# Projecting the gates in two token halves, with the sample's preparation dealt out between the tiles of the second

## The chip, the core and the metric

The kernel runs on one core of one Trainium2 chip. The metric is the device time of one execution in microseconds (us). A core has TensorE (PE: matrix products, its weight loads are shown as PEld), VectorE (DVE), ScalarE (ACT), GpSimd (POOL) and SyncE (SP), which only issues DMAs. Each engine works through its own queue in order and waits on semaphores. SBUF is the memory on the chip, PSUM the banks that TensorE writes.

## The reference, cut to what matters

The kernel computes one layer for a prompt of 2048 tokens and for a sample of 8 requests with one new token each. Both go through the same projection, and the sample then attends to a paged cache of 16,384 tokens.

```python
D_MODEL = 1024; SEQ = 2048; DEC_BATCH = 8; HEAD_DIM = 128; Q_LORA = 384; KV_LORA = 256; MLA_ROPE = 64; N_MEM = 256
IN_SIZES = (RET_W, RET_W, RET_W, Q_LORA, KV_LORA, MLA_ROPE, MEM_W, D_MIX)      # 512 512 512 384 256 64 512 1536

def project(h, pos, norm_g, w_in, qnorm_g, w_uq, w_uk, kvnorm_g):
    z = rms_norm(h, norm_g) @ w_in
    rq, rk, rv, cq, ckv, kpe, mq, gate = _split_cols(z, IN_SIZES)
    rq = rope(rq.reshape(B, T, RET_HEADS, HEAD_DIM), pos)
    rk = rope(rk.reshape(B, T, RET_HEADS, HEAD_DIM), pos) * (HEAD_DIM ** -0.5)
    q = jnp.einsum('btc,chd->bthd', rms_norm(cq, qnorm_g), w_uq)
    q_nope = q[..., :MLA_NOPE]
    q_pe = rope(q[..., MLA_NOPE:], pos)
    q_lat = jnp.einsum('bthd,chd->bthc', q_nope, w_uk)
    ckv = rms_norm(ckv, kvnorm_g)
    kpe = rope(kpe, pos)
    ...
# the sample: retention of one token per request, and memory attention over 256 rows per request
S = S * s_dec + k v^T ;  o = q S                     # state_ret (8, 4, 128, 128)
mem_o = mem_attend(mq, cache_mem_k[l], cache_mem_v[l])    # each (8, 256, 4, 128)
```

## The kernel before, in words

The work runs in stages, each a block in which all engines have their own program, with a barrier and a clearing of semaphores between two blocks (`Room.clear`, L82). The stages around the change are three.

**The projection** (`project`, L165 to L665). The prompt's rows stand turned in SBUF, split in a high part `xh` and a low part `xl`, each 128 x 8 x 2048 numbers, together 128 KB of each partition. The weights come in 17 stripes of 256 columns (`STRIPES`, L120): 3 and 2 stripes of the kind "N", 4 of the kind "R" (rotated), with 16 tiles each, and 8 of the kind "T" with 8 tiles each, of which 2 are memory queries and 6 are gates. A T tile is 128 columns of the weights by 512 tokens: 24 matmuls (L616), three products for each of 8 chunks. GpSimd loads the next stripe into `raw`, ScalarE copies its high part to `wh` (L404), VectorE subtracts for `wl` (L485). A tile goes to PSUM bank n % 4; ScalarE writes even tiles to `stage` (L421), VectorE odd ones (L517), and SyncE stores each pair (L332). In each stripe TensorE also projects the sample's 8 rows: `sample_rows`, a group of 16 matmuls (L631) after one tile and one of 2 (L638) some tiles later (`rows_at`, L138); VectorE copies the results out and SyncE stores them to `s_zs` (L339).

**The sample's preparation** (`sample_prepare`, L2370 to L2826), a block of its own. It reads `s_zs` back, normalises, rotates, projects the queries (`w_uq`, `w_uk`), builds the page indices and lets GpSimd gather the first step of the paged cache (L1802, L1804), adds k v^T to the states (`outer` on TensorE L2704, `new_state` on VectorE L2527), reads them with the queries (L2719), computes memory scores on VectorE (`spread` on TensorE L2712, `memory_scores` L2534 and L2537), their softmax, the memory values (L2819) and a head norm. All states (2 MB), memory keys (4 MB) and memory values (4 MB) are loaded whole.

**The sample's attention and the prompt's retention** (`sample_attention_and_retention`, from L1808), which starts with the tiles in `keep` (indices, queries, the first gathered rows).

Of the kernel before, what the change touches and what calls it, by code (L numbers as in the profile page):

```python
# [28 lines left out]
P = 128  # L29
# [24 lines left out]
class Count:  # L54


    def __init__(self, base=0):
        self.at = base
# [51 lines left out]
def rms_scale(dve, link, x, square, stat, n):  # L110
# [11 lines left out]
           + [("N", O_RV + c, SW) for c in range(0, W3, SW)] + [("T", NAT + c, SW) for c in range(0, TRN, SW)])  # L122
# [10 lines left out]
def tiles_of(stripe):  # L133

    return stripe[2] // P * (SEQ // 512) if stripe[0] == "T" else BLOCKS


def rows_at(s):  # L138

    return ROWS_AT if s == 0 else (1, 4)  # L140
# [24 lines left out]
def project(nc, t):  # L165
# [6 lines left out]
    with ExitStack() as ctx:  # L172
        r = Room(nc, ctx, "pj")
        xh = r.sb("xh", [P, KD, SEQ], F32R)
        xl = r.sb("xl", [P, KD, SEQ], F32R)
        raw = r.sb("raw", [P, 2, KD, SW])
        wh = [r.sb("wh0", [P, KD, SW], F32R)]
        wl = [r.sb("wl0", [P, KD, SW], F32R)]
        stage = r.sb("stage", [P, 2, 2, 512])
        xsT = r.sb("xsT", [P, KD, DEC])  # L180
        parts = r.sb("parts", [P, DEC])
        rows4 = r.sb("rows4", [P, SW])
        rows = r.sb("rows", [DEC, SW])
        kv = stage[:, :, :, :].rearrange("p b x n -> p b (x n)")
        mem_gain = kv[:, 1, :]
        with ExitStack() as early:
            def first(name, shape, dt=F32):
                return early.enter_context(nc.sbuf_tensor(f"pn_{name}", shape, dt))

            xmT = first("xmT", [P, KD, NMEM])  # L190
            kT = first("kT", [P, HEADS, NMEM])
            gain = first("gain", [P, D])
            x = first("x", [P, 4, D])
            ident = first("ident", [P, P])
            square = first("square", [P, D], mybir.dt.bfloat16)
            total = first("total", [P, 2 * PAIRS])
            half = first("half", [P, 2])
            stat = first("stat", [P, 2, 2, 2])
        wh.append(r.sb("wh1", [P, KD, SW], F32R))
        wl.append(r.sb("wl1", [P, KD, SW], F32R))  # L200
        rot = r.sb("rot", [P, 2, 2, HD + HD // 2])
        by_cos = r.sb("by_cos", [P, 2, HD])
        by_sin = r.sb("by_sin", [P, 2, HD])
        turned = r.sb("turned", [P, 2, 2, HD])
        decay = r.sb("decay", [P, 2 * HEADS])
# [3 lines left out]
        ps_row = r.ps("ps_row", [DEC, 512])  # L209
        (consts, mem_gain_in, gain_in, sum_ok, xn_ok, xT_ps, xm_ok, hi_ok, lo_ok, xs_ok, kv_out, w_hi, w_lo, mm_ok, clear_ok, row4_ps, row4_ok,  # L210
         row_ps, row_ok, row_out, ev_act, ev_dve, chain, mean_ok, root_ok, turned_ok, decay_in, parts_in, kT_out) = [r.sem(n) for n in (
            "consts mem_gain_in gain_in sum_ok xn_ok xT_ps xm_ok hi_ok lo_ok xs_ok kv_out w_hi w_lo mm_ok clear_ok row4_ps row4_ok "
            "row_ps row_ok row_out ev_act ev_dve chain mean_ok root_ok turned_ok decay_in parts_in kT_out").split()]
# [12 lines left out]
        TURNS = 2 * SAMPLE + 1  # L226

# [8 lines left out]
        with nc.Block() as block:  # L236
            @block.gpsimd
            def _(pool):
# [18 lines left out]
                for s, (kind, c0, w) in enumerate(STRIPES):  # L257
                    if s < 2:
                        pool.wait_ge(mm_ok, MEM_TILES - 2 + 2 * s)
                    else:  # L260
                        pool.wait_ge(w_lo, s - 1)
                        pool.wait_ge(row4_ps, s - 1)
                    pool.dma_start(raw[:, s % 2, :, 0:w], w_rows[:, :, c0:c0 + w]).then_inc(w_in[s % 2], 16)
                    for q in ((MEM_STRIPES + 1,), range(MEM_STRIPES + 2, PAIRS))[s] if s < 2 else ():
                        root_of(q)

            @block.sync
            def _(sp):
# [46 lines left out]
                for s, (kind, c0, w) in enumerate(STRIPES):  # L315
                    if s == 1:
# [4 lines left out]
                        load_rotation(1)  # L321
                    for n in range(first_tile[s], first_tile[s + 1], 2):
# [7 lines left out]
                        if kind == "T":  # L330
                            m, c = u // 4, u % 4
# [5 lines left out]
                        if u == rows_at(s)[1] // 2 * 2:  # L337
                            sp.wait_ge(row_ok, s + 1)
                            sp.dma_start(t["s_zs"][:, c0:c0 + w], rows[:, 0:w]).then_inc(row_out, 16)  # L339
# [5 lines left out]
                sp.wait_ge(row_out, 16 * len(STRIPES))  # L345
# [6 lines left out]
            def factor(s):  # L352
                return -MEM_SCALE if STRIPES[s][0] == "T" and STRIPES[s][1] < O_GATE else 1.0
# [16 lines left out]
            def _(act):  # L370
# [7 lines left out]
                def high_part(b):  # L378

                    for half in range(1 if b == SAMPLE else 2):  # L380
# [7 lines left out]
                        else:  # L388
                            act.copy(xh[:, chunk, (b - 2) * P:(b - 1) * P], ps_t[:, h % 2, :, :]).then_inc(hi_ok, 1)

                def early_tile(n):
                    act.wait_ge(mm_ok, n + 1)
                    to, w = early_target(n)
                    act.copy(to, ps[:, n % QUAD, 0:w]).then_inc(ev_act, 1)
# [11 lines left out]
                def tile(s, n):  # L406
# [10 lines left out]
                    elif n % 2 == 0:  # L417
                        stage_free(act, n)
                        act.wait_ge(mm_ok, n + 1)
                        w_tile = 512 if kind == "T" else w  # L420
                        act.activation(stage_view(n, w_tile), ps[:, n % QUAD, 0:w_tile], ACT.Copy, scale=factor(s)).then_inc(ev_act, 1)  # L421
# [26 lines left out]
                for s in range(1, len(STRIPES)):  # L448
                    if s + 1 < len(STRIPES):
                        split(s + 1)  # L450
                    for n in range(first_tile[s], first_tile[s + 1]):
                        tile(s, n)

            @block.vector
            def _(dve):
# [14 lines left out]
                def low_part(b):  # L470
                    for half in range(2):
                        h = 2 * (b - 2) + half
                        at = slice(half * HALF, (half + 1) * HALF), slice((b - 2) * P, (b - 1) * P)
                        dve.wait_ge(hi_ok, h + 1)
                        dve.tensor_tensor(xl[:, at[0], at[1]], ps_t[:, h % 2, :, :], xh[:, at[0], at[1]], ALU.subtract).then_inc(lo_ok, 1)
# [2437 lines left out]
```

## Time and profile before

| what | us |
|---|---|
| three runs | 2301.97 (median), 2296.97 to 2302.07 |
| the profiled execution | 2294.27, its span 2292.5 |
| last matmul of the projection starts | 861.57 |
| first instruction of the preparation's block | 866.63 |
| first instruction of the block after it | 942.36 |

Positions are us from the start of the span. The span is cut on the page into 40 slices of 57.3 us. PEclk is the granted clock of TensorE: 1.00 is 2.4 GHz, 0.50 is 1.2 GHz.

### The profile page before, as it was taken

To read this page: it belongs to the slowest core of one execution; us is meant where nothing else is said; L and a number is where in the kernel's file an instruction comes from. 1 tells how busy PE (TensorE), PEld (TensorE's weight loads), DVE (VectorE), ACT (ScalarE), POOL (GpSimd) and SP (SyncE) were. 2 spreads that over 40 slices of the span, in tenths; PEclk is the share of its full clock that TensorE was granted. 3 is DMA by queue.
4 is the path that set the end of the run, shared out by engine and by line. 5 is a ranking of instruction groups with operands and counts; after the bars stand their busy time and mean duration, and the time that the engine had idled before them with its cause. 6 is when DMAs were issued, how large, how long until landed. Compare 5 with 4: busy or idle time off the path is not lost. (4 is left out here: it accounts for less than half of the span.)

```text
span 2292.5 us, 48413 instructions
## 1 busy us (share of the span) xinstructions
PE 2124.3 (93%) x20401; PEld 1782.8 (78%) x20401; DVE 1278.5 (56%) x2736; ACT 653.1 (28%) x1478; POOL 223.9 (10%) x289
## 2 busy tenths in 40 slices
PE   7999999999999997599999999859899999899998
PEld 6999999997777775376677677648788888768886
DVE  4412444111111105599999999866577777655555
ACT  5311222100010001033333343434345545421110
POOL 1000000000000001122222222111222010000000
PEclk9999999999999995699999999979999999999999
DMA  7322332211112117799999999579997282154452
GB/s 255 112 74 78 100 99 89 83 61 65 65 65 83 46 47 245 295 364 363 369 378 371 374 366 377 202 252 308 349 212 137 48 148 99 50 191 138 160 161 83
DMA packets 185067, 421.94 MB, mean 184 GB/s; under 512 B 15072, under 2 KB 104320, under 8 KB 176664
## 3 DMA queue, kind: packets, MB, share of 16 engines
q0 software_dynamic: 44992, 234.56, 31.1%
q1 hardware_dynamic: 139872, 184.46, 24.0%
q8 instruction: 154, 2.52, 0.4%
q14 instruction: 49, 0.40, 0.1%
HBM read 325.48 MB, written 93.30 MB: 183 GB/s over the span
## 5 line engine op out<-in xcount | busy, mean ns | idle before, releaser
L618 PE MATMUL pj_ps<-pj_wh,pj_xh 128*128 128x256 f32 (+1 forms) x1152 | 326.1, 283 | 2.8 <-issue 2.8
L618 PE MATMUL pj_ps<-pj_wh,pj_xl 128*128 128x256 f32 (+1 forms) x1152 | 323.6, 281 | 0.0
L618 PE MATMUL pj_ps<-pj_wl,pj_xh 128*128 128x256 f32 (+1 forms) x1152 | 323.5, 281 | 0.0
L517 DVE TENSOR_SCALAR pj_stage<-pj_ps 128x256 f32<-128x256 f32 (+2 forms) x72 | 38.5, 535 | 483.1 <-PE pj_ps L616 314.2
L618 PEld LDWEIGHTS pj_ps<-pj_wh,pj_xh 128*128 128x128 f32 x1152 | 219.6, 191 | 10.6 <-issue 10.1
L2196 PE MATMUL sa_ps_s<-sa_turned,keep_q 128*32 128x128 f32 x5120 | 183.7, 279 | 47.5 <-DVE sa_turned L1972 44.2
L1972 DVE STREAM_TRANSPOSE sa_turned<-sa_nat 128x2048 f32<-128x2048 f32 x96 | 220.0, 2291 | 13.4 <-DMA sa_kp<-cache_kpe,keep_index 13.4
L618 PEld LDWEIGHTS pj_ps<-pj_wh,pj_xl 128*128 128x128 f32 x1152 | 219.7, 191 | 0.0
L618 PEld LDWEIGHTS pj_ps<-pj_wl,pj_xh 128*128 128x128 f32 x1152 | 219.7, 191 | 0.0
L616 PE MATMUL pj_ps<-pj_xh,pj_wh 128*128 128x512 f32 x512 | 202.7, 396 | 0.0
L616 PE MATMUL pj_ps<-pj_xl,pj_wh 128*128 128x512 f32 x512 | 201.0, 393 | 0.0
L616 PE MATMUL pj_ps<-pj_xh,pj_wl 128*128 128x512 f32 x512 | 200.9, 392 | 0.0
L2196 PEld LDWEIGHTS sa_ps_s<-sa_turned,keep_q 128*32 128x32 f32 x5120 | 132.8, 111 | 77.9 <-DVE sa_turned L1972 59.0
L421 ACT ACTIVATE pj_stage<-pj_ps 128x256 f32<-128x256 f32 (+2 forms) x72 | 34.1, 473 | 481.3 <-PE pj_ps L616 302.0
L1363 DVE TENSOR_TENSOR la_pl<-la_ps_p,la_ph 128x512 fp32r<-128x512 f32 (+1 forms) x144 | 88.4, 656 | 72.0 <-ACT la_ph L1409 72.0
L616 PEld LDWEIGHTS pj_ps<-pj_xh,pj_wh 128*128 128x128 f32 x512 | 96.1, 188 | 27.8 <-issue 6.9
L1400 ACT ACTIVATE la_row<-la_row,la_soft 128x128 f32<-128x128 f32 (+7 forms) x64 | 77.2, 1207 | 127.9 <-DVE la_soft L1350 127.9
L616 PEld LDWEIGHTS pj_ps<-pj_xl,pj_wh 128*128 128x128 f32 x512 | 96.1, 188 | 21.8
L616 PEld LDWEIGHTS pj_ps<-pj_xh,pj_wl 128*128 128x128 f32 x512 | 96.2, 188 | 21.0
L2220 PE MATMUL sa_ps_o<-sa_nat,sa_p_turned 128*16 128x256 f32 x1536 | 94.3, 379 | 4.4 <-issue 4.4
L1342 DVE CUSTOM_DVE_ANT_0 la_row<-la_ps_s,begin_causal 128x512 f32<-128x512 f32 (+3 forms) x160 | 92.3, 605 | 9.7 <-PE la_ps_s L1466 9.7
L1409 ACT CAST la_ph<-la_ps_p 128x512 fp32r<-128x512 f32 (+1 forms) x144 | 74.3, 565 | 39.5 <-PE la_ps_p L1479 38.6
(450 smaller groups left out, 4281.1 us busy)
## 6 DMA issues: line engine op xcount, KB each, us to landing
pj_raw<-w_in POOLq DMA_DIRECT2D x16, 1024.0 KB, 6.4
s_zn<-pj_stage SPq DMA_DIRECT2D x64, 256.0 KB, 2.2
s_zt<-pj_stage SPq DMA_DIRECT2D x32, 512.0 KB, 2.6
rm_z<-s_zn SPq DMA_DIRECT2D x16, 768.0 KB, 9.6
pn_x<-x_prompt SPq DMA_DIRECT2D x16, 512.0 KB, 3.8
s_k<-lp_st SPq DMA_DIRECT2D x16, 512.0 KB, 8.2
s_v<-lp_st SPq DMA_DIRECT2D x32, 256.0 KB, 5.3
s_qn<-lp_st SPq DMA_DIRECT2D x16, 512.0 KB, 5.1
```

The source lines that it names most:

```text
L421: act.activation(stage_view(n, w_tile), ps[:, n % QUAD, 0:w_tile], ACT.Copy, scale=factor(s)).then_inc(ev_act, 1)
L517: dve.tensor_scalar(stage_view(n, w_tile), ps[:, n % QUAD, 0:w_tile], factor(s), None, ALU.mult).then_inc(ev_dve, 1)
L616: mm = pe.matmul(ps[:, n % QUAD, :], wt[:, k, m * P:(m + 1) * P], of[:, k, c * 512:(c + 1) * 512], **flags)
L618: mm = pe.matmul(ps[:, n % QUAD, 0:w], of[:, k, u * P:(u + 1) * P], wt[:, k, 0:w], **flags)
L1342: dve.tensor_tensor_reduce(out=row[:, s, q, c * P:(c + w) * P], in0=ps_s[:, (at + n) % 3, 0:w * P], in1=m, scale=1.0, scalar=-3.0e38, op0= ...
L1363: dve.tensor_tensor(pl[:, n % RING, 0:w], ps_p[:, n % RING, 0:w], ph[:, n % RING, 0:w], ALU.subtract).then_inc(pl_ok, 1)
L1400: act.activation(row[:, s, q, 0:n], row[:, s, q, 0:n], ACT.Exp, bias=soft[:, s, q, 1:2], scale=MLA_SCALE, accum_out=soft[:, s, q, 2:3]).th ...
L1409: act.copy(ph[:, n % RING, 0:w], ps_p[:, n % RING, 0:w]).then_inc(ph_ok, 1)
L1972: dve.transpose(turned[:, s, a:z, :, :].rearrange("p c x q -> p x c q"), of.rearrange("p x (c q) -> p x c q", q=QR)).then_inc(t_ok, 1)
L2196: mm = pe.matmul(ps_s[j * QR:(j + 1) * QR, s, 0:TQ * QR], q32[:, u, c, :], turned[:, s, c, j * TQ:(j + 1) * TQ, :].rearrange("p x q -> p ( ...
L2220: mm = pe.matmul(ps_o[j * QR:j * QR + ROWS_Q, 0:KVL], p_turned[:, s, x, j, :], nat[g % DEEP][:, TQ * j + x, :], start=(x == 0), stop=(x == ...
```

## The change

The six gate stripes are projected twice over half of the tokens each: first all six for tokens 0 to 1023 (kind "T0", 4 tiles a stripe), then all six for tokens 1024 to 2047 (kind "T1"). So each gate stripe's weights are loaded and split twice. `xh` and `xl` are two tensors each, one per half; the first halves stand on the right side of SBUF and are given up when the T0 tiles are done. In that memory lie the tiles of the preparation, which is no block of its own any more: the class `SamplePrepare` has one method for each engine, called with k after tile k of the 24 T1 tiles ("slot" k). Tiles of T1 use two PSUM banks in turn, and the preparation the other six. The states are handled in two halves of 4 requests, and memory keys and values pass one request at a time through a ring of two buffers. The sample's gate rows are projected in T0, after tiles 0 and 2 of a stripe.

```diff
-           + [("N", O_RV + c, SW) for c in range(0, W3, SW)] + [("T", NAT + c, SW) for c in range(0, TRN, SW)])
+           + [("N", O_RV + c, SW) for c in range(0, W3, SW)] + [("T", O_MQ + c, SW) for c in range(0, W3, SW)]
+           + [(half, O_GATE + c, SW) for half in ("T0", "T1") for c in range(0, MIX, SW)])
...
-        xh = r.sb("xh", [P, KD, SEQ], F32R)
-        xl = r.sb("xl", [P, KD, SEQ], F32R)
+            xh, xl = [[front_half.enter_context(nc.sbuf_tensor(f"pj_{n}0", [P, KD, HALF_SEQ], F32R, side="right")),
+                       r.sb(f"{n}1", [P, KD, HALF_SEQ], F32R)] for n in ("xh", "xl")]
...
+        def bank_of(n):
+            return n % QUAD if n < late else late % QUAD // 2 * 2 + (n - late) % 2
...
                     if n >= QUAD:
-                        evacuated(pe, n - QUAD, free)
+                        evacuated(pe, n - 2 if n >= late + 2 else n - QUAD, free)
...
+                    if s >= LATE + 2:
+                        sample.pool(s - LATE - 2, pool)
...
-                        for i in range(2):
-                            evacuated(sp, n + i, staged)
+                        evacuated(sp, n, staged)
+                        if s >= LATE:
+                            sample.sync(n - late, sp)
+                        evacuated(sp, n + 1, staged)
...
                     for n in range(first_tile[s], first_tile[s + 1]):
                         tile(s, n)
-                        sample_rows(s, n - first_tile[s])
+                        if s >= LATE:
+                            sample.tensor(n - late, pe)
+                        else:
+                            sample_rows(s, n - first_tile[s])
...
+        if k == -1:
+            self.turned_over(sp)
+            self.zs_written(sp)
...
+        if 4 <= k <= 9:
+            sp.wait_ge(self.kq_ok, k - 3)
+            load_memory("cache_mem_k", k - 2)
+        if k == 5:
+            sp.wait_ge(self.cq_ps, 1)
+            sp.wait_ge(self.q4_ok, 2)
+            for n in range(QUADS):
+                for i in range(QUADS):
+                    sp.dma_start(self.q_in[i * QR:(i + 1) * QR, :, n, :], ...)
...
+        if 14 <= k <= 19:
+            sp.wait_ge(self.mo_ps, k - 13)
+            load_memory("cache_mem_v", k - 12)
...
+        if k == 1:                          # TensorE
+            self.banks_free(pe)
+            pe.wait_ge(self.ident_in, 16)
+            pe.wait_ge(self.cqn_ok, 1)
...
+        if 4 <= k <= 11:
+            spread(k - 4)
+        if k == 7:
+            pe.wait_ge(self.pick_in, 16)
+            pe.wait_ge(self.prod_ok, 1)
...
+            outer(0)
+            outer(1)
+        if k == 8:
+            outer(2)
+            outer(3)
+        if k == 9:
+            retention(0)
...
+        if 14 <= k <= 21:
+            memory_values(k - 14)
+        if k == 22:
+            pe.wait_ge(self.rows_ok, 2)
+            pe.wait_ge(self.cats_ok, 1)
+            turn_rows().then_inc(self.moT_ps, 1)
```

On TensorE the preparation's products stood together in a block of their own. Before (`sp_` names are tiles of the preparation, `sp_bank` its PSUM banks):

```order
L2763 MATMUL sp_bank<-keep_ident,sp_q_lat 128x128 x2
L2767 MATMUL sp_bank<-keep_ident,sp_qk 128x8 x4
L2712 MATMUL sp_bank<-sp_zs,sp_one_row 128x512
L2704 MATMUL sp_bank<-sp_zs,sp_k_only 128x128 x4
L2775 MATMUL sp_bank<-sp_psum,sp_pick 128x8 x4
L2704 MATMUL sp_bank<-sp_zs,sp_k_only 128x128 x4
L2712 MATMUL sp_bank<-sp_zs,sp_one_row 128x512
```

Now the same kinds stand between tiles; this is slot 7, the fullest, with the last two matmuls of tile 7 and the first of tile 8:

```order
L675 MATMUL pj_ps<-pj_xh,pj_wl 128x512
L675 MATMUL pj_ps<-pj_xl,pj_wh 128x512
L2867 MATMUL pj_ps_t<-sp_zm,sp_one_row 128x512
L2953 MATMUL pj_ps_row4<-sp_psum,sp_first 128x8 x4
L2856 MATMUL pj_ps<-sp_zq 128x128 x8
L675 MATMUL pj_ps<-pj_xh,pj_wh 128x512
```

The products are the same ones; what moved is that 24 matmuls of a tile stand between one slot's and the next's. (One product of these f32 shapes is two MATMUL records in the trace.)

On VectorE, this is what now stands in the queue from slot 5's end to slot 8 (`pj_stage<-pj_ps` writes out an odd tile, `pj_wl` is the split of a stripe's weights, `sp_rows<-sp_ring` and `sp_sm` are the memory scores, `sp_weights<-sp_weights` the states):

```order
L2672 TENSOR_REDUCE sp_sm<-sp_rows 128x2x4
L2669 TENSOR_TENSOR sp_rows<-sp_ring,pj_ps_t 128x1024
L2672 TENSOR_REDUCE sp_sm<-sp_rows 128x2x4
L2715 TENSOR_TENSOR sp_prod<-sp_q,sp_newT 128x32 x3
L2718 TENSOR_REDUCE sp_psum<-sp_prod 128x32
L571 TENSOR_SCALAR pj_stage<-pj_ps 128x512
L2669 TENSOR_TENSOR sp_rows<-sp_ring,pj_ps_t 128x1024
L2672 TENSOR_REDUCE sp_sm<-sp_rows 128x2x4
L2723 TENSOR_TENSOR sp_kept<-pj_ps_row,sp_mine 128x8
L2725 TENSOR_REDUCE keep_low<-sp_kept 128x2
L2660 SCALAR_TENSOR_TENSOR sp_weights<-sp_weights,pj_ps 128x128 x8
L539 TENSOR_TENSOR pj_wl<-pj_raw,pj_wh 128x2048
```

Before, the same work stood behind the block's start with no tile and no split in between; now each odd tile's way out of PSUM is queued behind the slot before it.

## Rows read from the trace of the kernel before

**Rows 1.** The page: 40 slices of the span, busy tenths and granted clock.

```profile
PE   7999999999999997599999999859899999899998
...
PEclk9999999999999995699999999979999999999999
```

**Rows 2.** Windows: stretch, length, busy time of each engine, granted clock, DMA share, GB/s.

```profile
760.00:861.96 101.96, 101.96 (x463) 80.39 (x462) 9.31 (x13) 7.29 (x10) 0.00 (x0) 1.00 0.12 47
861.96:875.66 13.70, 0.00 (x1) 0.03 (x1) 4.36 (x20) 0.00 (x0) 3.71 (x8) 0.65 0.56 168
875.66:930.00 54.34, 46.34 (x222) 30.34 (x222) 35.41 (x82) 10.17 (x24) 5.34 (x6) 0.50 0.90 292
930.00:935.70 5.70, 5.64 (x129) 5.14 (x129) 3.63 (x20) 0.00 (x1) 0.00 (x0) 0.63 0.14 52
935.70:938.10 2.40, 1.33 (x13) 0.98 (x9) 0.00 (x0) 1.16 (x4) 0.60 (x1) 1.00 0.03 7
```

**Rows 3.** Timeline around the two block ends: start, length, instruction.

```profile
861.57 0.39 PE L616 MATMUL pj_ps<-pj_xl,pj_wh 128*128 128x512 f32 x1
...
862.83 0.34 SPq L332 DMA_DIRECT2D s_zt<-pj_stage  x1
...
866.63 0.30 SPq L2450 DMA_DIRECT2D sp_zs<-s_zs  x1
...
942.36 0.36 SPq L1907 DMA_DIRECT2D rm_z<-s_zn  x1
```

**Rows 4.** Timeline of ScalarE, even tiles of one T stripe, two of the next.

```profile
545.33 0.60 ACT L421 ACTIVATE pj_stage<-pj_ps 128x512 f32<-128x512 f32 x1 [3.54 <-PE pj_ps L616]
557.44 0.60 ACT L421 ACTIVATE pj_stage<-pj_ps 128x512 f32<-128x512 f32 x1 [11.51 <-PE pj_ps L616]
568.32 0.60 ACT L421 ACTIVATE pj_stage<-pj_ps 128x512 f32<-128x512 f32 x1 [10.28 <-PE pj_ps L616]
579.96 0.60 ACT L421 ACTIVATE pj_stage<-pj_ps 128x512 f32<-128x512 f32 x1 [11.04 <-PE pj_ps L616]
...
603.38 0.60 ACT L421 ACTIVATE pj_stage<-pj_ps 128x512 f32<-128x512 f32 x1 [11.78 <-PE pj_ps L616]
614.58 0.60 ACT L421 ACTIVATE pj_stage<-pj_ps 128x512 f32<-128x512 f32 x1 [10.60 <-PE pj_ps L616]
```

**Rows 5.** Timeline of TensorE: the sample's two groups in one T stripe.

```profile
827.26 1.05 PE L631 MATMUL pj_ps_row<-pj_raw,pj_xsT 128*8 128x256 f32 x16
844.81 0.60 PE L638 MATMUL pj_ps_row<-pj_rows,pj_parts 128*8 128x256 f32 x2
```

**Rows 6.** Timeline, the preparation's start.

```profile
871.48 0.55 DVE L2551 CUSTOM_DVE_ANT_0 sp_square<-sp_zs 8x384 f32<-8x384 f32 x1 [8.72 <-DMA sp_gains<-mla_kvnorm_g]
...
876.46 0.21 DVE L2522 TENSOR_TENSOR sp_kpx<-sp_cos,sp_sin 8x64 f32<-8x64 f32 x1
```

**Rows 7.** Groups by form, 862 to 942 us: count, busy, mean ns, idle before.

```profile
L2712 PE MATMUL sp_bank<-sp_zs,sp_one_row 8*128 8x512 f32 x16 | 16.1, 1105 | 0.0
L2704 PE MATMUL sp_bank<-sp_zs,sp_k_only 8*128 8x128 f32 x64 | 15.5, 423 | 0.0
L2537 DVE TENSOR_REDUCE sp_sm<-sp_kq 128x8 f32<-128x1024 f32 x8 | 9.8, 1220 | 0.3
L2534 DVE TENSOR_TENSOR sp_kq<-sp_mem_k,sp_bank 128x1024 f32<-128x1024 f32 x8 | 9.7, 1219 | 8.8 <-PE sp_bank L2712 8.8
L2527 DVE SCALAR_TENSOR_TENSOR sp_state<-sp_state,sp_bank 128x128 f32<-128x128 f32 x32 | 7.0, 281 | 2.5 <-PE sp_bank L2704 2.3
```

**Rows 8.** The splits of a stripe's weights: count, duration ns min/median/max.

```profile
L404 ACT CAST pj_wh<-pj_raw x17: 1482/1905/1912, 54.0 to 769.8; 128x2048 fp32r<-128x2048 f32 x16, 128x1536 fp32r<-128x1536 f32 x1
L485 DVE TENSOR_TENSOR pj_wl<-pj_raw,pj_wh x17: 1759/2292/2293, 57.1 to 771.8; 128x2048 fp32r<-128x2048 f32 x16, 128x1536 fp32r<-128x1536 f32 x1
```

**Rows 9.** Timeline of SyncE: two series of small DMAs.

```profile
874.25 1.35 SPq L2468 DMA_DIRECT2D sp_gn<-ret_gn_g  x4
...
890.65 19.46 SPq L2481 DMA_DIRECT2D sp_q_in<-sp_q  x16
```

More of the change, by code:

```diff
@@ L162, in project_plan, with project @@
     return free, staged, rot_pairs, turned_before
-def project(nc, t):
+def project(nc, t, hold):
     with ExitStack() as ctx:
         r = Room(nc, ctx, "pj")
-        xh = r.sb("xh", [P, KD, SEQ], F32R)
-        xl = r.sb("xl", [P, KD, SEQ], F32R)
[L176 to L205, printed above, removed]
@@ new lines, in project, with first, turning @@
+        with ExitStack() as front_half:
+            xh, xl = [[front_half.enter_context(nc.sbuf_tensor(f"pj_{n}0", [P, KD, HALF_SEQ], F32R, side="right")),
+                       r.sb(f"{n}1", [P, KD, HALF_SEQ], F32R)] for n in ("xh", "xl")]
+            raw = r.sb("raw", [P, 2, KD, SW])
+            wh = [r.sb("wh0", [P, KD, SW], F32R)]
+            wl = [r.sb("wl0", [P, KD, SW], F32R)]
+            stage = r.sb("stage", [P, 2, 2, 512])
+            xsT = r.sb("xsT", [P, KD, DEC])
+            parts = r.sb("parts", [P, DEC])
+            rows4 = r.sb("rows4", [P, SW])
+            rows = r.sb("rows", [DEC, SW])
+            kv = stage[:, :, :, :].rearrange("p b x n -> p b (x n)")
+            mem_gain = kv[:, 1, :]
+            with ExitStack() as early:
+                def first(name, shape, dt=F32):
+                    return early.enter_context(nc.sbuf_tensor(f"pn_{name}", shape, dt))
+                xmT = first("xmT", [P, KD, NMEM])
+                kT = first("kT", [P, HEADS, NMEM])
+                gain = first("gain", [P, D])
+                x = first("x", [P, 4, D])
+                ident = first("ident", [P, P])
+                square = first("square", [P, D], mybir.dt.bfloat16)
+                total = first("total", [P, 2 * PAIRS])
+                half = first("half", [P, 2])
+                stat = first("stat", [P, 2, 2, 2])
+            wh.append(r.sb("wh1", [P, KD, SW], F32R))
+            wl.append(r.sb("wl1", [P, KD, SW], F32R))
+            with ExitStack() as middle:
+                def turning(name, shape):
+                    return middle.enter_context(nc.sbuf_tensor(f"pj_{name}", shape, F32))
+                rot = turning("rot", [P, 2, 2, HD + HD // 2])
+                by_cos = turning("by_cos", [P, 2, HD])
+                by_sin = turning("by_sin", [P, 2, HD])
+                turned = turning("turned", [P, 2, 2, HD])
+                decay = turning("decay", [P, 2 * HEADS])
@@ L226, in project, with turned_over, sample_banks_free, sample_rows_out @@
         TURNS = 2 * SAMPLE + 1
+        late = first_tile[LATE]
+        keep = Keep(nc, hold)
+        def bank_of(n):
+            return n % QUAD if n < late else late % QUAD // 2 * 2 + (n - late) % 2
+        def turned_over(eng):
+            eng.wait_ge(mm_ok, late)
+        def sample_banks_free(pe):
+            for n in range(late - QUAD, late):
+                if bank_of(n) not in (bank_of(late), bank_of(late + 1)):
+                    evacuated(pe, n, free)
+            pe.wait_ge(row_ok, LATE)
+        def sample_rows_out(eng):
+            eng.wait_ge(row_out, 16 * GATES)
+        def gate_rows_out(eng):
+            eng.wait_ge(gate_out, 16 * (LATE - GATES))
+        early_banks = [b for b in range(QUAD) if b not in (bank_of(late), bank_of(late + 1))]
+        sample = SamplePrepare(nc, t, ctx, r, keep, rows4, rows,
+                               [ps[:, b, :] for b in early_banks]
+                               + [ps_t[:, j, :, :].rearrange("p k q -> p (k q)") for j in range(2)] + [ps_row4[:, :], ps_row[:, :]],
+                               turned_over, sample_banks_free, sample_rows_out, gate_rows_out)
         def evacuated(eng, n, table):
@@ L321, in _ @@
                         load_rotation(1)
+                    if s == LATE:
+                        sample.sync(-1, sp)
                     for n in range(first_tile[s], first_tile[s + 1], 2):
@@ L452, in _ @@
                         tile(s, n)
+                        if s >= LATE:
+                            sample.scalar(n - late, act)
             @block.vector
@@ L559, in _ @@
                         tile(s, n)
-                        sample_rows(s, n - first_tile[s])
+                        if s >= LATE:
+                            sample.vector(n - late, dve)
+                        else:
+                            sample_rows(s, n - first_tile[s])
             @block.tensor
@@ L591, in memory_tile @@
                     for k in range(KD):
[L592 removed]
+                        mm = pe.matmul(ps[:, bank_of(n), 0:SW], xmT[:, k, b * P:(b + 1) * P], raw[:, m % 2, k, :], start=(k == 0),
                                        stop=(k == KD - 1))
@@ L637, in sample_rows @@
                             pe.wait_ge(row_ok, s)
-                        pe.matmul(ps_row[:, 0:w], parts[:, :], rows4[:, 0:w], start=True, stop=True).then_inc(row_ps, 1)
+                        pe.matmul(ps_row[0:DEC, 0:w], parts[:, :], rows4[:, 0:w], start=True, stop=True).then_inc(row_ps, 1)
                 pe.wait_ge(consts, 16)
@@ L664, in _ @@
                         tile(s, n)
-                        sample_rows(s, n - first_tile[s])
+                        if s >= LATE:
+                            sample.tensor(n - late, pe)
+                        else:
+                            sample_rows(s, n - first_tile[s])
+    return keep
 class Mark:
@@ L2890, in build @@
     t.update((name, nc.dram_tensor(name, shape, F32, kind="Internal").ap()) for name, shape in SCRATCH + PARTS)
-    project(nc, t)
-    with ExitStack() as ctx:
-        keep = Keep(nc, ctx)
-        sample_prepare(nc, t, keep)
+    with ExitStack() as hold:
+        keep = project(nc, t, hold)
         sample_attention_and_retention(nc, t, keep)
```

983 lines of the change are left out of this document (529 added, 454 removed).

## The prediction

> **What bounds the kernel now.** I read the slices of the page first. Through the projection TensorE is at 9 tenths in nearly every slice at full clock; in the 16th and 17th slice (860 to 974) the busy row falls to 7 and 5 and the clock row to 5 and 6 [rows 1]. The windows then show what these two slices are: from 861.96 to 938.10 TensorE does only the sample's preparation, first 13.70 us with nothing at all, then 54.34 us of which it is busy 46.34, at a clock of 0.50, which is 1.2 GHz [rows 2]. VectorE is busy 35.41 of the same 54.34. Last, the timeline gives the edges: the projection's last matmul ends at 861.57 + 0.39 = 861.96, the next block starts at 866.63, the one after it at 942.36 [rows 3]. So there are 80.4 us between the projection's last product and the sample's attention. The projection in front of it is bound by TensorE alone: in 760 to 861.96 TensorE is busy 101.96 of 101.96, VectorE 9.31 and ScalarE 7.29 [rows 2]. Whatever goes between its tiles on VectorE, ScalarE or a DMA queue can be free; whatever TensorE does there is paid in full.
>
> **What goes.** The preparation's block goes from its first instruction to that of the next: 942.36 - 866.63 = 75.7 us. The 4.7 us from the last product to the start of the next block (last tile out, its store, the barrier) stay, once.
>
> **What stays the same.** 48 gate tiles of 24 matmuls before and after. A pair of T tiles without other work takes 568.32 - 557.44 = 10.88 us, 5.44 a tile [rows 4]. The sample's two groups are still done once in each of the 8 stripes.
>
> **What is added off the path.** Six more loads of a stripe (1 MB) and six more pairs of splits, 1.91 us on ScalarE and 2.29 on VectorE [rows 8]. A stripe of four tiles lasts 4 x 5.44 = 21.8 us, and its split stands one stripe ahead; 4.2 us of 21.8 are hidden. In T0 I cost them at nothing. If the cover were gone, the whole would be 6 x 4.2 = 25 us.
>
> **What is added on TensorE.** The preparation's products now run between dense tiles, so at full clock. The three windows give 46.34 at 0.50, 5.64 at 0.63 and 1.33 at 1.00 [rows 2]: 23.2 + 3.6 + 1.3 = 28.1 us at full clock. Then each change from tile to small group costs something that busy time doesn't hold. The sample's own groups show it: a group busy 1.05 us [rows 5] stretches a pair to 557.44 - 545.33 = 12.11, by 1.23; one of 0.60 stretches the pair to 11.64, by 0.76 [rows 4]. That is 0.17 over the busy time. 22 of the 24 slots hold work, many in more than one group behind a wait of its own. From below 22 x 0.17 = 3.7; from above, for twice as many groups at twice the price, 15. I take 5, thirty groups at 0.17.
>
> **Waits inside the slots.** I walk the queues with t = 0 at the end of the last T0 tile. SyncE stores that pair and the row, and issues the first three loads by 3 us. In the block before, VectorE began 871.48 - 866.63 = 4.9 us after the first load's issue and had the rotated key 5.2 us later [rows 3, 6]. Here it starts at about 6.6 and is done at 11.8, and then waits for the 15th load, issued at 8, which may land between 10 and 14. Tile 1 ends at 10.9, so TensorE stands in slot 1 for up to 3 us; I take 2. Queued behind VectorE's wait is tile 1's way out of PSUM, which is only needed by tile 3 at 16.3 or later.
>
> The fullest part is slots 4 to 12. Per slot VectorE has memory scores, 1.22 + 1.22, in four of them two states' updates, 8 x 0.22 = 1.7 (7.0 us for 32 [rows 7]), and a split of 2.29 at tiles 4, 8 and 12. The eight scores, eight states, three splits, the rotated query copies and four tiles out come to 19.5 + 7.0 + 6.9 + 1.6 + 2.8 = 38 us, in nine slots of 5.44 plus 1 to 3 us each, about 68 us. So VectorE has room, and its longest piece, in slot 7 (2.4 + 0.4 + 1.8 + 2.3 = 6.9 us), ends before tile 8's successor needs a bank. ScalarE's keys (8 of 0.72 us) have more. TensorE in slot 7: a spread of 2 records (16.1 us for 16 at half clock [rows 7], so 1.0 at full), the low products 0.9, two outers of 8 records (15.5 for 64, so 1.0 each): 3.9 us, with everything that it waits for done before tile 7 ends at about 53. SyncE's waits for scores (kq_ok) come about 3 us after a tile's end, and hold the store of a pair by that; the stage has a second buffer, two tiles of room. The block's idle TensorE time from 875.66 to 938.10, 62.44 - 53.31 = 9.1 us, is the upper bound for all waits together, the lower is nothing: 2, between 0 and 9.
>
> **The clock.** From 875.66 to 930 TensorE is busy 46 of 54 us and the granted clock stays at 0.50; it rises only in 930 to 935.7, when the memory values' products run [rows 2]. Most products before have 8 rows of input (`8*128` in the records [rows 7]). So such products, however busy, did not bring the clock back, and a slot full of them might count as a pause. The Trainium skill ("TensorE: Matmul & The Clock Gate", part 1) says that sustained matmul activity releases the throttle and an idle stretch brings it back; under "HAM oscillation" it tells of a kernel that ran its bursts cold every time because it waited between them, which speaks against this change. Taken by its words, busy slots would keep the clock and the sum would have no clock term; the row differs, since 46 busy us did not release it. I go by the row: slots 7, 8, 11 and 12 hold 3 to 4 us of such work, slot 1 a wait. After 861.96 the window to 875.66 has 0.65, so full clock for (0.65 - 0.5) x 2 x 13.7 = 4.1 us after the last product; and dense work at 930 had it back within (1 - 0.63) x 2 x 5.7 = 4.2 us [rows 2]. A fall costs at least 2.1 us, with a part of its slot perhaps 3.5. None to four falls: 0 to 14 us. I take 3, one fall.
>
> **The sum.** On TensorE + 28.1 + 5 + 2 + 3 = 38. Net 75.7 - 38 = 37.6 us less: 2294.27 - 37.6 = 2256.7 against the profiled execution (its span, 2292.5, plus 1.8). The median of the three runs, 2301.97, lies 7.7 above that execution, so the runs should show 2264.4; I say 2264.
>
> After the last slot with work (22) there is still tile 23, 5.44 us, over which the sample's rows are copied and stored, so the handover isn't later. The sample's attention then starts as before, with its first rows long gathered. TensorE pauses there as it did, so its clock starts as low.
>
> **The rivals.**
>
> - *The slots wait on each other.* T1's tiles have two banks, not four, and each odd tile's copy is behind a slot's work on VectorE. If every one of slots 4 to 12 held TensorE for the scores of its own slot (2.4 us, 9 slots = 22) the time were 2286. For: queues are strictly in order and the scores stand before the copy. Against: the walk above leaves 3 us or more a tile. 8%.
> - *SyncE is late.* The 16 small query loads took 19.46 us of its queue before, against 1.35 for four others, 0.34 each [rows 9]; with 4 MB of memory values and more in front of them in flight. At that price slot 5's series ends near t = 62, the keys for slot 8 come about 4 us late, and some of it reaches TensorE's spreads; the stores wait too. Some 8 us: 2272. For: the number. Against: here only 0.5 MB pieces are in flight. 12%.
> - *Layout.* A pair in the next stripe, with the other weight buffers, takes 614.58 - 603.38 = 11.20 and not 10.88 [rows 4], 0.16 a tile, and nothing on the engines explains it. Every tile of SBUF moves now. If all 64 T tiles had the one or the other, 32 x 0.16 = 5 us either way: 2259 or 2269. I have it in the range only.
> - *The clock stays low in T1 (slower).* If falls in the slots outlast the tiles, each tile costs 5.44 us more. From 7 tiles on (37.6 / 5.44 = 6.9) the gain is gone; half of the 24 at half clock gives 2264 + 65 = 2329. For: the clock at 0.50 through 46 busy us. Against: a tile is 5.4 us or, at half clock, 10.9 of the densest work of the kernel, and such work had it back in 4.2. 4%.
> - *It doesn't do what it says.* If the preparation outran the 24 tiles, its rest would stand behind them at half clock: with a third of it, 20 us, 2284. The slots are fixed in each queue, so this needs the last loads or stores to be late. 3%.
>
> **How the numbers follow.** My forecast with its own bounds has 73%: TensorE's part between 28.1 + 3.7 = 32 and 28.1 + 10 + 5 + 7 = 50, so 2258 to 2276 on the median, with the layout 2253 to 2281. The two rivals on the same side add 2272 to 2286. The lower end takes in that the runs before already spread from 2297. Range 2250 to 2287. Under 0.3% (7 us) a measurement of this kernel can't tell a difference from none. Faster by more (under 2295): the forecast, the two same-side rivals, layout and nearly all of the outrun, 94%. Within 0.3%: 2%. Slower: 4%.
>
> **What the changed profile would show.** The clock row should have no 5 before the attention; the last gate matmul should end at 861.96 + 38 = about 900, and the next block start 4.7 us behind it. T0 should take 24 x 5.44 us plus 6 times the sample's groups, T1 131 + 38 = 169. Windows over T1 should give a clock of 0.95 or more; TensorE's idle should stand in slot 1. DVE waits for loads above 2 us in slots 5 to 12 would speak for the second rival. T1 over 180 us with a clock at 1.00 would prove me wrong on waits, a clock under 0.9 on the clock.

## The result, and the profile after

The changed kernel takes 2286.47 us (median of 6 runs, 2277.97 to 2288.52) where the one before takes 2301.18 (6 runs, 2296.97 to 2305.70): a ratio of 0.9941, 95% interval 0.9923 to 0.9959, 14.7 us less. Two later sets gave 0.9909 (0.9891 to 0.9927) and 0.9908 (0.9885 to 0.9930). The median of all 16 runs is 2281.6, so the change is worth about 20 us. The forecast was 2264, 37.6 less: the direction was right, but the first set shows less than half of the forecast gain, and all sets together about half.

The page's slices show the gap of [rows 1] closed: TensorE stays at 9 tenths through slice 16, and the clock row has one 7 in the place of a 5 and a 6. The 6 that is left in TensorE's row (slice 17, 917 to 974) is the handover and the start of the attention.

```profile
PE   7999999999999999698999989869899999989998
...
PEclk9999999999999999799999999969999999999999
```

The windows answer [rows 2]. The first is T0, then T1 (the 24 tiles with the preparation between them), three pieces of T1, the handover, and the attention's block.

```profile
581.65:726.30 144.65, 144.65 (x685) 109.81 (x684) 25.62 (x29) 18.62 (x18) 6.18 (x7) 1.00 0.27 95
...
726.30:916.66 190.36, 186.05 (x935) 143.68 (x933) 62.99 (x139) 28.01 (x46) 13.55 (x19) 0.95 0.45 144
740.00:750.20 10.20, 7.97 (x23) 6.25 (x24) 4.92 (x9) 1.07 (x2) 0.00 (x0) 0.51 0.69 225
790.00:806.00 16.00, 16.00 (x68) 12.46 (x66) 9.20 (x22) 5.27 (x6) 2.15 (x2) 0.79 0.56 188
834.00:842.00 8.00, 8.00 (x44) 6.19 (x46) 1.93 (x8) 0.28 (x1) 1.15 (x1) 0.79 0.45 131
916.66:921.94 5.28, 0.00 (x0) 0.00 (x0) 0.69 (x1) 0.00 (x0) 0.00 (x0) 0.88 0.24 99
921.94:1492.38 570.44, 503.56 (x10456) 389.93 (x10456) 506.61 (x908) 201.64 (x657) 118.24 (x126) 0.96 0.89 341
```

T0 is 144.65 us with TensorE busy throughout and the clock at 1.00, 2 us over what its tiles and the sample's rows were put at: the doubled splits are hidden. T1 is 190.4 us, not the forecast's 169, and TensorE idles only 4.3 of them. The clock was at half for 0.98 x 10.2 + 0.42 x 16 + 0.42 x 8 = 20 us (a stretch at a mean clock c spends the share 2 x (1 - c) at half). The ends show that the handover is 5.3 us, as expected, and that the next block starts 20.4 us earlier than in [rows 3]:

```profile
916.27 0.39 PE L675 MATMUL pj_ps<-pj_xl,pj_wh 128*128 128x512 f32 x1
...
921.94 0.33 SPq L1973 DMA_DIRECT2D rm_z<-s_zn  x1
```

In T1 the waits are those of slot 1, in the timeline of TensorE and VectorE:

```profile
737.71 0.20 PE L2907 MATMUL pj_ps<-keep_ident,pj_rows 8*128 8x8 f32 x1
740.25 1.97 PE L2911 MATMUL pj_ps_t<-keep_ident,sp_ring 128*128 128x128 f32 x8 [2.34 <-DMA sp_ring<-w_uk]
744.19 0.27 PE L2914 MATMUL pj_ps_row<-keep_ident,sp_pages_f 64*16 64x64 f32 x1 [1.97 <-DVE sp_pages_f L2689]
...
743.97 0.17 DVE L2689 CAST sp_pages_f<-sp_pages 64x16 f32<-64x16 int32 x1 [7.41 <-DMA keep_pull<-c_pull]
```

The groups by form over T1 answer [rows 7] and give what the forecast did not expect, the memory values (L2887): 128 records that were busy 5.64 us before [rows 2] now take 15.5.

```profile
L2887 PE MATMUL pj_ps<-sp_ring,sp_turns 128*32 128x128 f32 x128 | 15.5, 274 | 0.0
...
L2867 PE MATMUL pj_ps_t<-sp_zm,sp_one_row 8*128 8x512 f32 x16 | 9.0, 640 | 0.0
L2856 PE MATMUL pj_ps<-sp_zq 8*128 8x128 f32 x64 | 8.3, 278 | 0.0
```

The splits are as long as in [rows 8], 23 of them in place of 17. The 16 query loads took 10.54 us of SyncE's queue, against 19.46 in [rows 9], and nothing on TensorE waited for them.

```profile
L539 DVE TENSOR_TENSOR pj_wl<-pj_raw,pj_wh x23: 1757/2292/2294, 57.0 to 860.8; 128x2048 fp32r<-128x2048 f32 x22, 128x1536 fp32r<-128x1536 f32 x1
...
776.69 10.54 SPq L2582 DMA_DIRECT2D sp_queries<-sp_q  x16
```

### The profile page after: what moved, and what is told of

Its sections match the earlier page's. It is cut to its first block and busy times, and to the rows that moved or that the text cites. A ratio compares the mean times of both kernels' runs of the same rounds, so it can differ in the third digit from the quotient of the medians.

```text
span 2285.4 us, 48464 instructions
## 1 busy us (share of the span) xinstructions
PE 2135.5 (93%) x20401; PEld 1791.2 (78%) x20401; DVE 1293.5 (57%) x2743; ACT 666.0 (29%) x1484; POOL 230.3 (10%) x295
## 5 line engine op out<-in xcount | busy, mean ns | idle before, releaser
L675 PE MATMUL pj_ps<-pj_xh,pj_wh 128*128 128x512 f32 x512 | 208.2, 407 | 0.0
```

The lines of the kernel that those rows point to most:

```text
L675: mm = pe.matmul(ps[:, bank_of(n), :], wt[:, k, m * P:(m + 1) * P], of[c // 2][:, k, c % 2 * 512:(c % 2 + 1) * 512], **flags)
```

## The experiments

Runs of one kernel spread over some 12 us, so the place of an edit is read from each profile as well. Two marks serve: the length from the first small product of slot 1 to the last gate matmul (T1 without its first 11 us; the forecast's 169 is 158 by it), and the start of the attention's block. Each experiment on the changed kernel has four to six runs, and the intervals of the three single edits overlap that of the unchanged kernel of their set. So what one edit alone gives is read from the first mark; its share of the whole time is known only roughly. The start of the block carries, besides, what comes before T1: slot 1 begins anywhere from 736.5 to 739.8 us in these profiles.

| kernel | median us | ratio to before, 95% | slot 1 to last gate matmul | attention's block starts |
|---|---|---|---|---|
| before, first and second profile | 2301.18 | | | 942.36, 944.39 |
| changed, first | 2286.47 | 0.9941 (0.9923 to 0.9959) | 179.3 | 921.94 |
| changed, second | 2279.63 | 0.9909 (0.9891 to 0.9927) | 179.1 | 921.36 |
| changed, third | 2280.01 | 0.9908 (0.9885 to 0.9930) | 179.2 | 922.44 |
| changed, values in four groups | 2273.21 | 0.9871 (0.9850 to 0.9892) | 168.9 | 913.51 |
| changed, loads' work later | 2276.96 | 0.9883 (0.9860 to 0.9906) | 172.9 | 916.29 |
| changed, 128 rows | 2272.86 | 0.9881 (0.9847 to 0.9916) | 170.9 | 916.07 |
| changed, values and rows | 2264.41 | 0.9833 (0.9808 to 0.9857) | 160.5 | 902.30 |
| changed, all three | 2256.36 | 0.9797 (0.9774 to 0.9820) | 154.9 | 899.83 |
| before, values one after another | 2305.37 | 1.0026 (1.0005 to 1.0048) | | 951.43 |
| before, 128 rows | 2288.78 | 0.9958 (0.9945 to 0.9972) | | 933.32 |
| before, gates in halves | 2298.94 | 1.0001 (0.9987 to 1.0015) | | 942.02 |

**The two kernels again.** The changed one, unchanged, in two sets, and the one before with a second profile.

> The changed kernel unchanged, as the yardstick for the three others of this set. Its profile showed two stalls of about 2.5 us in the attention of the sample and that stage 12 us longer than before. Theory: such stalls are part of the kernel and come again at the same places, so the time is 2284 to 2289 and the stage is again about 575 us from its block's start to the next. Rival: they are chance, then the stage is near 563 us here and the execution 2275 or so.

> The kernel before, profiled once more, for the length of its stages. If the attention of the sample takes 563 us again where the changed kernel's takes 575, the difference belongs to the kernels; if the two overlap, it is chance.

> The changed kernel unchanged, in the same set, because its first runs lay 14.7 us and its second 22.2 us under before. Both profiles have the attention's block start 20 to 22 us earlier than in the runs of before, and the attention itself took 558 to 570 us in all profiles of either kind. Theory: the change is worth about 21 us and the rest is chance of that stage: ratio near 0.991. Rival: the change also lengthens the attention, by the 12 us of the first profile: ratio near 0.994 or above.

The attention's block, from its start to that of the next block, took 558.5 and 562.8 us in the two profiles of before and 570.4, 560.7 and 566.6 in the three of the changed kernel. Kernels of the old form gave 561.1, 562.0 and 570.3, the other new ones 563.0 to 570.1. So the 12 us that the first comparison of profiles shows in this block are mostly chance, as the rival of the first expectation had it, and what the change itself gives is the earlier start of the block, 20 to 23 us. The third set's ratio of 0.9908 agrees with that. The means are 563 (five profiles) and 566 (eight), with standard deviations of 4 and 3; whether the change costs some 3 us there stays open.

Nor does all of the earlier start come from the preparation. The 48 gate tiles begin earlier too, first before, then changed:

```profile
585.15 0.39 PE L616 MATMUL pj_ps<-pj_xh,pj_wh 128*128 128x512 f32 x1
```

```profile
581.40 0.39 PE L675 MATMUL pj_ps<-pj_xh,pj_wh 128*128 128x512 f32 x1
```

From there to the last product it is 276.8 us before and 335.3 in the changed kernel, 58.5 more. With the handover, 16.7 us of the 80.4 are saved; the other 3.7 of the 20.4 arose before the first gate tile. The three profiles of the changed kernel have this tile at 581.0 to 581.9, all profiles of the kernels of the old form at 585.1 to 587.0, the one with gates in halves included (585.10). So another part of the change must do it; which one was not tested.

**One part alone: gates in halves.** In the kernel before, the stripes were cut as in the changed one, the preparation left as its own block.

```diff
-           + [("T", NAT + c, SW) for c in range(0, TRN, SW)])
+           + [("T", O_MQ + c, SW) for c in range(0, W3, SW)]
+           + [(half, O_GATE + c, SW) for half in ("T0", "T1") for c in range(0, MIX, SW)])
```

> One part of the change alone: the six gate stripes are projected twice over half of the tokens, each with its own load and split of the weights, while the preparation stays a block of its own. Theory: 4.2 us of splits stand under 21.8 us of tiles, so the same time as before within 3 us. Rival: the split is in the way once a stripe (4.2 us each, or part of it), then 6 to 25 us slower.

2298.94 against 2298.96: no difference, and the attention's block starts where it did. The two halves take 276.83 us together, against 276.81 for the same tiles before: six further pairs of splits, all under tiles, cost nothing.

```profile
585.10:729.28 144.18, 144.18 (x685) 109.81 (x684) 25.64 (x29) 18.61 (x18) 6.19 (x7) 1.00 0.28 96
729.28:861.93 132.65, 132.65 (x577) 107.96 (x575) 20.09 (x18) 16.73 (x17) 2.65 (x3) 1.00 0.20 72
...
942.02 0.37 SPq L1917 DMA_DIRECT2D rm_z<-s_zn  x1
```

**The memory values.** First in the changed kernel: each head of a request gets its own 32 PSUM rows (and the copy in slot 22 reads them in that order).

```diff
-            for h in range(HEADS):
-                for m in range(MT):
-                    mm = pe.matmul((A, B)[b // HALF][32 * j:32 * j + 32, h * HD:(h + 1) * HD], ...
+            for m in range(MT):
+                for h in range(HEADS):
+                    mm = pe.matmul((A, B)[b // HALF][32 * h:32 * h + 32, j * HD:(j + 1) * HD], ...
```

> The four heads of a request's memory values write four different groups of 32 PSUM rows, and the group varies fastest, where all 16 records of a slot wrote one group. Theory 'column groups': the records of a slot run side by side again, 16 records in about 0.5 us instead of 1.87, over eight slots 10 to 11 us less: 10 to 11 us under the unchanged one. Rival 'slots': what the slots 14 to 21 cost is the change from tile to small products and back, not the records; then under 2 us less.

The same slot in the changed kernel and in this one, 16 records of the same shape:

```profile
864.50 1.94 PE L2887 MATMUL pj_ps<-sp_ring,sp_turns 128*32 128x128 f32 x16
```

```profile
857.34 0.65 PE L2888 MATMUL pj_ps<-sp_ring,sp_turns 128*32 128x128 f32 x16
```

1.29 us less in each of eight slots is 10.3; T1 is 10.2 shorter. The time is 6.4 less, not the 10 to 11 expected, but the two sets of four runs spread by 8.7 and 6.5 us. Then the other way round in the kernel before: the request outside, so that 16 records in a row write the same 32 rows.

```diff
-                    for h in range(HEADS):
-                        for m in range(MT):
-                            for j in range(4):
+                    for j in range(4):
+                        for h in range(HEADS):
+                            for m in range(MT):
```

> The kernel before with the memory values' products in another order: the request outside, head and chunk inside, so that 16 records after one another write the same 32 PSUM rows, as the changed kernel has them. Theory 'column groups': the 128 records take 15 us at full clock and more while the clock is still at half, instead of 5.64: 9 to 15 us slower than before. Rival: the order doesn't matter, same time within 2 us.

```profile
931.45 13.44 PE L2819 MATMUL sp_bank<-sp_mem_v,sp_pm_pad 128*32 128x128 f32 x128 [0.36 <-ACT sp_pm_pad L2685]
```

```profile
930.05 5.71 PE L2819 MATMUL sp_bank<-sp_mem_v,sp_pm_pad 128*32 128x128 f32 x128 [0.36 <-ACT sp_pm_pad L2685]
```

The first line is this kernel, the second the one before: 7.7 us more for the same 128 records. The block after starts 951.43 against 942.4 and 944.4, 7 to 9 later, and the median is 6.4 above. That is under the expected 9 to 15, and far from the rival's "same time"; the theory stands in both directions.

**The rows of the products.** Spreading and outer products have 8 input rows. Both kernels got 128 rows for them, 120 of zeros: their tiles are 128 partitions high, cleared by a memset, and the 8 true rows are loaded into them later. The code is cut from the changed kernel, where `k_only` is a view of `zq`; in the kernel before the same is done to `zs`, `one_row` and `k_only`. The kernel before comes first.

```diff
-        self.zq = sb("zq", [DEC, 3 * W3])
-        self.zm = sb("zm", [DEC, W3])
-        self.one_row = sb("one_row", [DEC, DEC, P])
+        self.zq = sb("zq", [P, 3 * W3])
+        self.zm = sb("zm", [P, W3])
+        self.one_row = sb("one_row", [P, DEC, P])
```

> The kernel before with 128 input rows (120 of them zeros) for the spreading and the outer products of the preparation. Theory 'rows': the preparation stayed at a granted clock of 0.50 from 875 to 930 although TensorE was busy 46 of 54 us, because most products had 8 rows; with 128 rows the clock comes back on the way and the preparation is 8 to 20 us shorter. Rival: the clock stays at 0.50 as before; then the same time, or 1 to 2 us slower for the later start of some loads.

```profile
875.00:930.00 55.00, 36.12 (x356) 24.13 (x356) 37.34 (x96) 11.41 (x28) 6.39 (x8) 0.83 0.94 302
...
886.80:917.40 30.60, 20.47 (x168) 14.02 (x168) 26.91 (x58) 7.32 (x15) 3.77 (x3) 1.00 1.01 321
```

The kernel before had 0.50 all through this stretch with TensorE busy 46 of 54 us [rows 2]. Now the clock is at 1.00 from 886.8 to 917.4 although TensorE is busy only 20.5 of 30.6. The order of the products is the same. The attention starts 9 to 11 us earlier and the time is 10.2 less, half of what the whole change brings.

> The products of 8 input rows (the spreading of the memory queries and the outer products) are given 128 rows, of which 120 are zeros; their columns and their number are the same. Theory 'rows': slots 7, 8 and 12 lose the clock because 8 rows don't count as work; with 128 rows these three falls of 3.4 us go, about 5 us less. Rival 'waits': the falls come from TensorE's idle moments in or before those slots; then nothing changes, within 2 us, or it is 1 to 2 us slower for the later loads.

Then in the changed kernel. The window over the tiles behind slots 7 and 8 has the clock at 1.00 now, where the unchanged one shows 0.79:

```profile
790.00:806.00 16.00, 16.00 (x85) 13.21 (x85) 10.26 (x24) 5.28 (x6) 2.15 (x2) 1.00 0.68 219
```

The Trainium skill ("TensorE: Matmul & The Clock Gate", part 1) has the clock follow how busy the engine has been. By that rule slots 7 and 12, where TensorE did not idle at all, would have kept it. The changed kernel disagrees (0.79), this one agrees (1.00): the products differ between them only in their rows. The fall in slot 1 is there in both (0.77 from 738 to 753 with 128 rows), behind the waits for loads.

T1 became 8.2 us shorter, more than the 5 expected for the clock; the time is 6.8 less. The rest is at the edges between a tile and a small group. Slot 6 holds one spread, first in the changed kernel (second profile), then with 128 rows:

```profile
779.53 0.39 PE L675 MATMUL pj_ps<-pj_xl,pj_wh 128*128 128x512 f32 x1
779.85 1.12 PE L2867 MATMUL pj_ps_t<-sp_zm,sp_one_row 8*128 8x512 f32 x2
780.90 0.50 PE L675 MATMUL pj_ps<-pj_xh,pj_wh 128*128 128x512 f32 x1
781.23 0.40 PE L675 MATMUL pj_ps<-pj_xh,pj_wl 128*128 128x512 f32 x1
```

```profile
781.74 0.39 PE L675 MATMUL pj_ps<-pj_xl,pj_wh 128*128 128x512 f32 x1
781.96 1.02 PE L2872 MATMUL pj_ps_t<-sp_zm,sp_one_row 128*128 128x512 f32 x2
782.42 0.79 PE L675 MATMUL pj_ps<-pj_xh,pj_wh 128*128 128x512 f32 x1
783.05 0.39 PE L675 MATMUL pj_ps<-pj_xh,pj_wl 128*128 128x512 f32 x1
```

With equal rows the spread starts 0.22 us after the last matmul, as another matmul would; with 8 rows 0.32 after it. From the tile's last start to the second matmul behind the spread it is 781.23 - 779.53 = 1.70 us with 8 rows and 783.05 - 781.74 = 1.31 with 128. The Trainium skill ("TensorEngine Tiling (Array Packing)", Key Properties) says that a change of the array's mode drains the engine. The 0.4 us agree with that if 8 rows put the array in another mode than 128, which the profile does not show.

**The waits of slot 1.** What waits for `w_uk` and for the last of the 15 loads (the turning of `w_uk`, the page numbers, and what follows from both) moves one slot later.

```diff
         if k == 1:                                     # TensorE
...
-            pe.wait_ge(self.uk_in, 16)
...
-            pe.transpose(E[0:GP, 0:STEPS], self.pages_f[:, :], ...).then_inc(self.index_ps, 1)
         if k == 2:
...
+            pe.wait_ge(self.uk_in, 16)
...
+            pe.transpose(E[0:GP, 0:STEPS], self.pages_f[:, :], ...).then_inc(self.index_ps, 1)
```

> The turning of w_uk and of the page numbers, and with them the copy of the turned w_uk, the page indices and the first two loads of memory keys, stand one slot later. Theory: slot 1's 4.3 us of waits for loads go, and with them the clock fall that follows at 740 (10.2 us at half clock, 5 us lost), so 4 to 9 us less than the unchanged one. Rival: the next slot waits for the same loads or the keys come late, and the time is the same within 2 us; or the fall comes anyhow, then only the 4.

```profile
738.41 0.20 PE L2909 MATMUL pj_ps<-keep_ident,pj_rows 8*128 8x8 f32 x1
744.34 1.18 PE L2915 MATMUL pj_ps_row<-sp_weights,sp_cqT 128*32 128x192 f32 x24
745.45 1.09 PE L2921 MATMUL pj_ps_t<-keep_ident,sp_ring 128*128 128x128 f32 x8
746.48 0.22 PE L2924 MATMUL pj_ps_row<-keep_ident,sp_pages_f 64*16 64x64 f32 x1
```

No wait is left in slots 1 and 2, and the same transposes take 1.09 us and not the 1.97 of the first profile (in the second they took 1.09 too, before the clock fell). With the wait the fall in slot 1 is gone. T1 is 6.2 us shorter; the time is 2.7 less, under the expected 4 to 9, and within the noise of four runs. The falls behind the 8-row slots are still there, as the windows of this kernel show; here the last one stands behind slot 11:

```profile
784.00:800.00 16.00, 16.00 (x61) 12.42 (x62) 8.00 (x20) 4.55 (x5) 2.15 (x2) 0.79 0.55 177
818.00:826.00 8.00, 8.00 (x27) 6.39 (x26) 5.77 (x11) 3.23 (x3) 0.00 (x0) 0.57 0.38 126
```

**Together.** The values and the rows, and all three.

> The same without the shift of the loads' work: heads in four PSUM groups and 128 input rows. If the causes are separate, the block starts near 908 and the time is 13 us under the unchanged kernel; slot 1 then holds the 4 us of waits and one clock fall behind it, and no other fall comes before the last gate tile. If the shift gives nothing beside the rows, this one equals the kernel with all three.

> Three edits together on the changed kernel: the memory values' heads in four PSUM groups, the work that waits for loads one slot later, and 128 input rows (120 of them zeros) for the spreading and the outer products. Alone they let the attention's block start at 913.5, 916.3 and 916.1 us where the unchanged one had 921.4: 7.9, 5.1 and 5.3 less. Theory 'three separate causes': they add up, the block starts near 903 and the time is 18 us under the unchanged kernel, near 2263. The second half of the gates then takes about 172 us of the forecast's 169. Rival: the clock is what two of them share, or another wait comes up in the slots, and the block starts no earlier than 908, 12 us under the unchanged one.

In length of T1 the causes add up: 10.2 + 8.2 + 6.2 = 24.6 us as three single edits, 24.2 together; for values and rows 18.4 as single edits and 18.6 together. Those two are 15.6 us under the unchanged kernel of the set, against 13 expected; the shift of the loads' work is worth another 8.1 in time and 2.5 in the start of the block, so it isn't covered by the rows. All three bring T1 to 154.9, three us under the forecast's 158, and the clock to 1.00 in all of it, though one wait of 1.89 us comes back in slot 2:

```profile
749.98 0.22 PE L2930 MATMUL pj_ps_row<-keep_ident,sp_pages_f 64*16 64x64 f32 x1 [1.89 <-DVE sp_pages_f L2700]
...
739.62:894.54 154.92, 153.02 (x888) 119.26 (x887) 54.53 (x112) 25.54 (x44) 10.47 (x12) 1.00 0.51 163
```

The time is 2256.36, 44 us under before and 23.6 under the changed kernel of the same set. That is more than the 18 of the theory and the 12 of its rival. This version is the fastest of all that were run.

## Why the prediction was half right

- **What goes, what stays.** Right. The halves alone cost nothing, and T0 took the 144.65 us here that it took there (144.18). The handover is 5.3 us against 4.7.
- **The sum on TensorE.** Here it failed: 190.4 us, which is 59 over the 131 of the tiles, against 38 forecast. The 21 us have three measured places, the memory values (12), the clock (6) and the waits (2); a fourth, the tiles themselves, is nearly made up by the edges.
- **The memory values, the largest.** The step "5.64 at 0.63", 3.6 us at full clock, took the duration of 128 records as their own. Those records ran with the request innermost, four neighbours writing four groups of PSUM rows side by side. One request a slot, as the ring of two buffers wants it, lets all 16 records write one group: 15.5 us in all. This is the step that failed: the term was put at 3.6 and measured 15.5, short by 12, and the edit takes back 10.3 of them. The order of the loops stood in both kernels' code.
- **The waits.** "I take 2" in slot 1; 4.3 came (2.34 + 1.97). The time of landing was off: the 15th load was issued at 734.87, 8.6 us behind the last T0 tile as foreseen, and landed just before 743.97, 9.1 us later and not 2 to 6. The first 2.34 us of the wait are for `w_uk`, 512 KB issued at 731.95, which the walk did not have. From 734 to 738 the DMA engines were full (share 1.01, 364 GB/s), so the loads probably stood behind one another; no run has them apart.

```profile
734.00:738.00 4.00, 3.92 (x21) 2.89 (x19) 2.32 (x12) 0.18 (x2) 0.82 (x2) 1.00 1.01 364
```

- **The clock.** The reasons were right (8-row products did not hold it, and slot 1 held a wait) and it was bounded by 0 to 14; I took one fall at 3. It was 20 us at half clock, of which TensorE idled 2.2, so 9 us were lost: one long stretch from slot 1 on and three falls behind slots 7, 8 and 12. A fall costs half of what TensorE is busy in it, 1.7 us for the short ones and 4 for the one behind the wait. The falls are not fixed to these slots: the third profile of the same kernel has one longer fall behind slot 7 and none behind slot 8, for nearly the same T1.
- **The tiles, and the small groups' edges.** I took 5 us for thirty edges, and 59.4 - 28.1 - 11.9 - 4.3 - 9 = 6 are left of the measured sum. But most of it is no edge. The 131 were 24 tiles at 5.44, the fastest pair of [rows 4]. In T1 a tile at full clock has its first and last matmul 5.35 to 5.47 us apart, which makes 5.6 to 5.7 for all 24:

```profile
781.51 0.50 PE L675 MATMUL pj_ps<-pj_xh,pj_wh 128*128 128x512 f32 x1
786.86 0.39 PE L675 MATMUL pj_ps<-pj_xl,pj_wh 128*128 128x512 f32 x1
...
874.19 0.50 PE L675 MATMUL pj_ps<-pj_xh,pj_wh 128*128 128x512 f32 x1
879.66 0.40 PE L675 MATMUL pj_ps<-pj_xl,pj_wh 128*128 128x512 f32 x1
```

  The mean is 5.64, so 24 tiles are 4.8 us over 24 x 5.44, and 1 to 2 us are left for the edges: the 5 were too many, and it is luck that the rest comes near them. The kernel before with gates in halves took 132.65 for the same 24 tiles, 5.53 each. Why tiles of one shape take 5.44 to 5.7 us no run shows. That an edge's price hangs on the rows I did not see.
- **What would prove it wrong.** T1 was over 180 with a clock of 0.95, so neither of the two marks (at 1.00, or under 0.9) was met. In 190 us a clock of 0.95 is already the 20 us at half; the mark of 0.9 was set too low, and the memory values were in no mark at all.
- **The rivals.** The slots did not wait on each other: 4.3 us of idle time, all in slot 1. SyncE was late for nobody. That the first set's 2286 is the price of the first rival is chance. Layout, which stood in the range only, went both ways: the T1 tiles are slower than those of the forecast, and the gate tiles began 3.7 us earlier, which the sum did not have; without that the forecast would have missed by more.

## What to carry to other kernels

When products are dealt out in smaller portions, look at what runs side by side in the old order: a duration read from a group in which four PSUM row groups take turns holds only as long as they do. Products with 8 input rows kept the array busy here without keeping its clock; filling them up to 128 with zero rows cost nothing on TensorE and was worth 10 us even in the old kernel. And what one edit gives is better read from the stage's own marks in each profile, since the time of the whole moves by chance as much as one such edit.

## What the runs showed of the hardware

- The same products with 128 input rows and with 8: clock 1.00 from 886.8 to 917.4 us with TensorE busy 20.5 of 30.6, against 0.50 from 875.7 to 930 with TensorE busy 46.3 of 54.3.
- 16 records of 128 columns to one 32-row group of PSUM: 1.94 us; to four in turn: 0.65. 128 such records: 13.44 us in groups of 16, 5.71 with the four in turn.
- A spread of two 8-row records between 128-row matmuls costs about 0.4 us more than the same with 128 rows (1.70 against 1.31).
- Tiles of 24 equal matmuls at full clock took 5.44 to 5.7 us, depending on the stripe and the kernel; the cause is open.
- The attention's block took 558.5 to 570.4 us over thirteen profiles with the same work in it, and 560.7 to 570.4 over three of one kernel.
